# Two blocks of a transformer on one core: the second mixer's block attention reordered in pairs of units

## The reference, cut to what matters

```python
def second_block(x, ...):
    u = rms_norm(x, pre_mix_g[l]) @ w_in[l]
    u_conf, u_sc, u_att, u_lru = jnp.split(u, splits, axis=-1)
    y_a = conformer_conv_mixer(u_conf, ...)   # gated, 31-tap depthwise conv, group norm, silu
    y_b = short_conv_mixer(u_sc, ...)
    y_c = moba_attention(u_att)               # 4 heads of 64; softmax(q k - slope * distance) v
    y_d = rglru_mixer(u_lru, ...)             # conv, two gates, a linear recurrence, gelu
    y = jnp.concatenate([y_a, y_b, y_c, y_d], axis=-1) @ w_out[l]
    ...
```

## Time and profile before

| | us |
|---|---|
| median of 3 runs | 1278.79 (1278.21 to 1279.44) |
| the profiled execution | 1277.38 |
| its span, first to last instruction | 1275.6 |
| TensorE busy | 1267.5 |
| DVE busy | 741.4 |
| ACT busy | 569.3 |
| mean granted TensorE clock | 0.999 of full speed |

### The profile page before, as it was taken

The page is one execution under the profiler, slowest core; times in us unless marked ns, Lnnn a source line. Parts: engine busy times, 40 slices in busy tenths (PEclk is TensorE's granted clock), DMA queues, the critical chain, the costliest instruction groups (busy, mean ns, idle before and its releaser), DMA issues.

```text
span 1275.6 us, 15978 instructions
## 1 busy us (share of the span) xinstructions
PE 1267.5 (99%) x6406; PEld 1066.0 (84%) x6406; DVE 741.4 (58%) x1091; ACT 569.3 (45%) x974; POOL 7.0 (1%) x8
## 2 busy tenths in 40 slices
PE   9999999999999999999999999999999999999998
PEld 9877888898888888888888898778888888888886
DVE  5888876675586555555533589777653333433333
ACT  5666643344445444444422364576343322322222
POOL 0000010000000000000000000000000000000000
PEclk9999999999999999999999999999999999999999
DMA  8445446122224333233532052123243332333311
GB/s 257 141 165 191 139 129 221 65 83 66 101 82 133 99 99 98 91 94 97 164 93 92 32 159 93 51 67 118 80 134 99 99 95 91 115 96 99 99 50 66
DMA packets 43521, 138.54 MB, mean 109 GB/s; under 512 B 4628, under 2 KB 10260, under 8 KB 43192
## 3 DMA queue, kind: packets, MB, share of 16 engines
q1 hardware_dynamic: 43016, 137.13, 33.4%
q10 hardware_dynamic: 432, 0.39, 0.1%
HBM read 131.74 MB, written 5.77 MB: 108 GB/s over the span
## 4 chain that ended last, share of the span: by engine, by line
PE 88%; DMA 1%; DVE 0%; ACT 0%; issue 0%; DVEq 0%
PE bank L1295 15%; PE bank L1297 15%; PE bank L1296 15%; PE bank L1436 5%; PE bank L1437 5%; PE bank L1440 5%; PE bank L1438 5%; PE bank L1441 5%; PE bank L1439 5%; PE bank L1515 1%; PE bank L1579 1%; PE bank L1417 1%; PE bank L1416 1%; PE bank L1415 1%; PE bank L1565 1%; PE bank L1638 0%
## 5 line engine op out<-in xcount | busy, mean ns | idle before, releaser
L1295 PE MATMUL bank<-xh,whi 128*128 128x512 f32 (+1 forms) x1136 | 413.8, 364 | 0.0
L1296 PE MATMUL bank<-xl,whi 128*128 128x512 f32 (+1 forms) x1136 | 409.9, 361 | 0.0
L1297 PE MATMUL bank<-xh,wlo 128*128 128x512 f32 (+1 forms) x1136 | 409.8, 361 | 0.0
L2163 DVE TENSOR_TENSOR wlo<-stage,whi 128x1024 fp32r<-128x1024 f32 (+1 forms) x222 | 267.4, 1210 | 228.7 <-ACT whi L1698 228.5
L1698 ACT CAST whi<-stage 128x1024 fp32r<-128x1024 f32 (+1 forms) x222 | 228.5, 1036 | 199.4 <-PE bank L1441 157.2
L1295 PEld LDWEIGHTS bank<-xh,whi 128*128 128x128 f32 x1136 | 214.4, 189 | 36.9 <-issue 4.8
L1297 PEld LDWEIGHTS bank<-xh,wlo 128*128 128x128 f32 x1136 | 214.4, 189 | 32.6
L1296 PEld LDWEIGHTS bank<-xl,whi 128*128 128x128 f32 x1136 | 214.5, 189 | 32.1 <-issue 0.2
L1436 PE MATMUL bank<-whi,xh 128*128 128x512 f32 x281 | 110.3, 393 | 0.1
L1437 PE MATMUL bank<-whi,xh 128*128 128x512 f32 x281 | 109.4, 389 | 0.0
L1438 PE MATMUL bank<-wlo,xh 128*128 128x512 f32 x281 | 109.4, 389 | 0.0
(11 more groups left out here) (339 smaller groups left out, 1404.1 us busy)
## 6 DMA issues: line engine op xcount, KB each, us to landing
stage<-in_W_m SPq DMA_DIRECT2D x64, 512.0 KB, 3.6
stage<-in_W_up SPq DMA_DIRECT2D x44, 512.0 KB, 3.6
stage<-in_W_down SPq DMA_DIRECT2D x22, 512.0 KB, 3.6
stage<-in_W_in_a SPq DMA_DIRECT2D x19, 512.0 KB, 3.9
stage<-in_W_out SPq DMA_DIRECT2D x16, 512.0 KB, 3.7
stage<-in_W_in_b SPq DMA_DIRECT2D x10, 512.0 KB, 3.6
stage<-in_W_kv_k SPq DMA_DIRECT2D x8, 512.0 KB, 3.5
stage<-in_W_kv_v SPq DMA_DIRECT2D x8, 512.0 KB, 3.7
```

The source lines that it names most:

```text
L1295: e.matmul(b[:, cols], hi[:, k, :], xh[:, k, cols], start=(k == 0), stop=False)
L1296: e.matmul(b[:, cols], hi[:, k, :], xl[:, k, cols], start=False, stop=False)
L1297: last = e.matmul(b[:, cols], lo[:, k, :], xh[:, k, cols], start=False, stop=(k == 7))
L2163: e.tensor_tensor(wlo[:, plan.place[i], c], stage[:, i % NSTAGE, c], whi[:, plan.place[i], c].bitcast(F32), ALU.subtract).then_inc(S["w_lo"])
```

## The change

The step `mb_score` is taken apart into its three engines: `mb_score` (TensorE's matmuls), `mb_logit` (DVE) and `mb_exp` (ACT), which can now stand at different places in the list. A new method `mb_scores(u)` puts the matmuls of units u and u + 1 side by side and then the logits of u; the second unit's logits, the Exps, norms and transposes follow in later slots, and the two products with v stand side by side again. The taps are spread anew (the same 60 in the same order), `lru_gates(1)` goes from slot 22 to 23, and `lru_gates(0)`, `lru_a`, `lru_b` and `cf_mean` keep their slots. Nothing of the arithmetic is changed.

By slot, with the place in the main stream after which it stands (f and b: front and back half of a projection; gates, lru_a, lru_b and the other non-attention steps are shown where they stand beside attention):

| slot | after | before | after the change |
|---|---|---|---|
| 6 | in2_v tile 0 | score 0 | scores 0, 1; logit 0 |
| 7 | tile 1 | | logit 1; exp 0 |
| 8 | tile 2 | norm 0; score 1 | norm 0; exp 1 |
| 9 | tile 3 | | turn 0; norm 1 |
| 10 | in2_d 0 f | turn 0; norm 1; score 2 | turn 1 |
| 11 | in2_d 0 b | | pv 0, 1; scores 2, 3; logit 2 |
| 12 | in2_d 1 f | norm 2; turn 1; pv 0; score 3 | logit 3; exp 2 |
| 13 | in2_d 1 b | | norm 2; exp 3 |
| 14 | in2_b 0 f | norm 3; turn 2; pv 1; score 4 | turn 2; norm 3 |
| 15 | in2_b 0 b | norm 4 | turn 3 |
| 16 | in2_b 1 f | turn 3; pv 2; score 5 | pv 2, 3; scores 4, 5; logit 4 |
| 17 | in2_b 1 b | pv 3; norm 5 | logit 5; exp 4 |
| 18 | in2_b 2 f | gates 0; turn 4; score 6 | norm 4; gates 0 |
| 19 | in2_b 2 b | | exp 5 |
| 20 | in2_b 3 f | norm 6; turn 5; pv 4; score 7 | turn 4; norm 5 |
| 21 | in2_b 3 b, lru_gelu | | turn 5 |
| 22 | in2_b 4 f | pv 5; norm 7; turn 6; gates 1 | pv 4, 5; scores 6, 7; logit 6 |
| 23 | in2_b 4 b, sc_c 0 | | logit 7; exp 6; gates 1 |
| 24 | in2_b 5 f | pv 6; turn 7; lru_a | norm 6; exp 7; lru_a |
| 25 | in2_b 5 b, sc_c 1 | cf_parts; lru_b | turn 6; norm 7; cf_parts; lru_b |
| 26 | in2_b 6 f | pv 7 | turn 7 |
| 27 | in2_b 6 b | cf_mean | pv 6, 7; cf_mean |

Before, "score" stands for matmuls, logits and Exps together. Splits stand between slots as before: 146 ahead of in2_b 0, 147 and 148 behind lru_in 0 and 1, 149, 150 and 151 ahead of in2_b 3, 4 and 5.

```diff
@@ -775,11 +775,13 @@
         for q in range(2):
             self.step("cf_scale", q)
 
-    def mb_score(self, u):
-        for e in range(2):
-            self.fill("mb_score", u, e)
-            self.out(("mb_score", u, e), "mb_logit", 2 * u + e + 1)
-        self.step("mb_score", u)
+    def mb_scores(self, u):
+        for v in (u, u + 1):
+            for e in range(2):
+                self.fill("mb_score", v, e)
+                self.out(("mb_score", v, e), "mb_logit", 2 * v + e + 1)
+            self.step("mb_score", v)
+        self.step("mb_logit", u)
 
     def mb_turn(self, u):
         n = sum(MOBA_BANKS[:u])
@@ -822,82 +824,89 @@
         tap(3)
         yield
 
-        self.mb_score(0)
+        self.mb_scores(0)
+        tap(1)
+        yield
+        self.step("mb_logit", 1)
+        self.step("mb_exp", 0)
         tap(2)
         yield
+        self.step("mb_norm", 0)
+        self.step("mb_exp", 1)
         tap(3)
         yield
-        self.step("mb_norm", 0)
-        self.mb_score(1)
-        tap(2)
-        yield
-        tap(3)
-        yield
-
         self.mb_turn(0)
         self.step("mb_norm", 1)
-        self.mb_score(2)
+        tap(3)
+        yield
+        self.mb_turn(1)
+        tap(3)
+        yield
+
+        self.mb_pv(0)
+        self.mb_pv(1)
+        self.mb_scores(2)
+        tap(1)
+        yield
+        self.step("mb_logit", 3)
+        self.step("mb_exp", 2)
+        tap(3)
+        yield
+        self.step("mb_norm", 2)
+        self.step("mb_exp", 3)
+        tap(3)
+        yield
+        self.mb_turn(2)
+        self.step("mb_norm", 3)
+        tap(3)
+        yield
+        self.mb_turn(3)
+        tap(3)
+        yield
+
+        self.mb_pv(2)
+        self.mb_pv(3)
+        self.mb_scores(4)
+        tap(1)
+        yield
+        self.step("mb_logit", 5)
+        self.step("mb_exp", 4)
         tap(2)
         yield
+
+        self.step("mb_norm", 4)
+        self.lru_gates(0)
         tap(3)
         yield
-        self.step("mb_norm", 2)
-        self.mb_turn(1)
-        self.mb_pv(0)
-        self.mb_score(3)
-        tap(2)
-        yield
-        tap(4)
-        yield
-
-        self.step("mb_norm", 3)
-        self.mb_turn(2)
-        self.mb_pv(1)
-        self.mb_score(4)
-        tap(2)
-        yield
-        self.step("mb_norm", 4)
+        self.step("mb_exp", 5)
+        tap(3)
+        yield
+        self.mb_turn(4)
+        self.step("mb_norm", 5)
+        tap(3)
+        yield
+        self.mb_turn(5)
+        tap(3)
+        yield
+
+        self.mb_pv(4)
+        self.mb_pv(5)
+        self.mb_scores(6)
         tap(1)
         yield
-        self.mb_turn(3)
-        self.mb_pv(2)
-        self.mb_score(5)
-        tap(2)
-        yield
-        self.mb_pv(3)
-        tap(1)
-        self.step("mb_norm", 5)
-        yield
-
-        self.lru_gates(0)
-        self.mb_turn(4)
-        self.mb_score(6)
-        tap(2)
-        yield
-        tap(3)
-        yield
-        self.step("mb_norm", 6)
-        self.mb_turn(5)
-        self.mb_pv(4)
-        self.mb_score(7)
-        tap(3)
-        yield
-        tap(3)
-        yield
-
-        self.mb_pv(5)
-        self.step("mb_norm", 7)
-        self.mb_turn(6)
+        self.step("mb_logit", 7)
+        self.step("mb_exp", 6)
         self.lru_gates(1)
         tap(3)
         yield
-        tap(4)
-        yield
-        self.mb_pv(6)
-        self.mb_turn(7)
+
+        self.step("mb_norm", 6)
+        self.step("mb_exp", 7)
         self.step("lru_a")
         tap(4)
         yield
+        self.mb_turn(6)
+        self.step("mb_norm", 7)
         tap(60)
         self.keep("cf")
         for q in range(2):
@@ -906,8 +915,10 @@
         self.step("lru_b")
         yield
 
+        self.mb_turn(7)
+        yield
+        self.mb_pv(6)
         self.mb_pv(7)
-        yield
         self.cf_mean()
         yield
         self.step("lru_scan")
@@ -2012,7 +2023,7 @@
                 for z in range(2):
                     e.copy(av[:, 2 * z:2 * z + 2, :], tiles(bank_of("in2_v", z)[:], 2)).then_inc(S["v2_out"])
 
-            def mb_score(u):
+            def mb_exp(u):
                 w = 128 * (units[u][1] + 1)
                 q.wait_ge(S["mb_m"], u + 1)
                 for z in range(2):
@@ -2137,7 +2148,7 @@
                         warm=warm, xq=xq, xa_k=xa_k, xa_v=xa_v, xa_exp=xa_exp, xa_turn=xa_turn, decay=decay,
                         xa_pv=xa_pv, up=up, rms_stats=rms_stats, rms_late=rms_late, ln_apply=ln_apply, last_norm=last_norm, cf_in=cf_in, cf_first=cf_first, cf_parts=cf_parts, cf_mean=cf_mean,
                         cf_var=cf_var, cf_exp=cf_exp, cf_gate=cf_gate, in2_a=in2_a, in2_v=in2_v,
-                        mb_score=mb_score, mb_norm=mb_norm, mb_turn=mb_turn, lru_in=lru_in, lru_gate=lru_gate,
+                        mb_exp=mb_exp, mb_norm=mb_norm, mb_turn=mb_turn, lru_in=lru_in, lru_gate=lru_gate,
                         lru_a=lru_a, lru_b=lru_b, lru_gelu=lru_gelu, sc_c=sc_c, sc_conv=sc_conv,
                         post_norm=post_norm, m1=m1, store=store)
             e.dma_start(XT[:, 0, X0[0]], d["xT"][0][:, X0[0]]).then_inc(S["ld_xf"], 16)
@@ -2585,7 +2596,7 @@
                 e.scalar_tensor_tensor(out=yT[:, c, :], in0=cq[c], scalar=1.0, in1=cy[c], op0=ALU.add, op1=ALU.mult
                                        ).then_inc(S["cf_y"])
 
-            def mb_score(u):
+            def mb_logit(u):
                 p, i = units[u]
                 w = 128 * (i + 1)
                 Lq = Lm[u % 3][:, :, 0:w]
@@ -2712,7 +2723,7 @@
                         xq=xq, xa_k=xa_k, xa_v=xa_v, xa_turn=xa_turn, xa_score=xa_score, xa_norm=xa_norm, decay=decay, xa_pv=xa_pv, up_setup=up_setup, up=up, eps=eps,
                         rms_apply=rms_apply, rms_late=rms_late, gain=gain, ln_sums=ln_sums, ln_apply=ln_apply,
                         last_norm=last_norm, cf_in=cf_in, cf_tap=cf_tap, cf_parts=cf_parts, cf_mean=cf_mean, cf_scale=cf_scale,
-                        cf_out=cf_out, mb_score=mb_score, mb_norm=mb_norm, mb_pv=mb_pv, lru_in=lru_in, lru_a=lru_a,
+                        cf_out=cf_out, mb_logit=mb_logit, mb_norm=mb_norm, mb_pv=mb_pv, lru_in=lru_in, lru_a=lru_a,
                         lru_b=lru_b, lru_scan=lru_scan, sc_x=sc_x, sc_conv=sc_conv, sc_b=sc_b, post_norm=post_norm,
                         m1=m1)
             for name, *a in plan.steps:
```

More of the change, by code:

```diff
@@ L859, in beside_mixer_two @@
         self.step("mb_norm", 4)
+        self.lru_gates(0)
[14 more added lines that the diff above has]
+        self.mb_scores(6)
         tap(1)
         yield
-        self.mb_turn(3)
-        self.mb_pv(2)
-        self.mb_score(5)
-        tap(2)
-        yield
-        self.mb_pv(3)
-        tap(1)
-        self.step("mb_norm", 5)
-        yield
-        self.lru_gates(0)
-        self.mb_turn(4)
-        self.mb_score(6)
-        tap(2)
-        yield
+        self.step("mb_logit", 7)
+        self.step("mb_exp", 6)
+        self.lru_gates(1)
         tap(3)
@@ L879, in beside_mixer_two @@
         self.step("mb_norm", 6)
-        self.mb_turn(5)
-        self.mb_pv(4)
-        self.mb_score(7)
-        tap(3)
-        yield
-        tap(3)
-        yield
-        self.mb_pv(5)
-        self.step("mb_norm", 7)
-        self.mb_turn(6)
-        self.lru_gates(1)
-        tap(3)
-        yield
-        tap(4)
-        yield
-        self.mb_pv(6)
-        self.mb_turn(7)
+        self.step("mb_exp", 7)
         self.step("lru_a")
```

## The result

The changed kernel takes 1282.8 us (median of 6 runs, 1281.6 to 1284.4) against 1278.3 for the kernel before (6 runs beside it): ratio 1.0038, 95% interval 1.0028 to 1.0048. It is slower by 4.5 us; 4.9 had been forecast. Its profiled execution took 1281.8, with a span of 1280.0 against 1275.6.

The account below looks back on a forecast made before the run. TensorE, busy 99% of the span, bounds the kernel: waits 1.4 + 0.3 + 2.6 + 1.6 = 5.9, less 1.0 of switching, gives +4.9 on 1277.4: 1282.3, or 1283.7 us on the runs' median scale; range 1280.5 to 1287.0.

Parts of the forecast that it names:

- The waits of turns 5, 6 and 7: Second mixer: TensorE's transposes of units 5, 6 and 7 wait 1.4, 0.3 and 2.6 us for ACT's mb_norm.
- turns 2, 3 and 4: Transposes on TensorE's way to turn 5, counted at 0.54, 0.32 and 0.97 us within its 28.6.
- pv 7: Unit 7's product with v: TensorE waits 1.6 us for ACT's copy of turn 7, behind cf_parts and lru_b.
- The clock: Rival: TensorE's granted clock falls during a wait, the longest counted being 2.6 us; chance under 2 in 100.
- The row from the span's end: Profile row cited against the clock rival: granted clock at 2.4 GHz through four microseconds without a matmul.
- The switching: TensorE in the second mixer: pairing saves entries, less three more returns to the main stream; net -1.0 us.
- Entries: Cost on TensorE of entering a kind of work, paid once per run: 0.21 us for scores, 0.15 for products with v.
- All pairs together: Entries saved on TensorE by four score pairs and four v pairs: 1.44 us.
- The three returns: Main stream broken in 15 slots instead of 12: three more returns at 0.15 us each, 0.45 at most.

Follow-up runs that it names:

- e2_tail: Changed kernel with the last pair's steps (Exp, norm, turns and products of units 6 and 7) put forward; 1277.6 us, ratio 0.9997 to the kernel before.
- e3_unit5: Changed kernel with mb_norm(5) one slot earlier (slot 19, behind the second tap); 1280.4 us, ratio 1.0024 to the kernel before.
- e4_both: Changed kernel with the edits of e2_tail and e3_unit5 together; 1276.3 us, ratio 0.9985 to the kernel before.
- e5_lru_a_behind: Changed kernel with lru_a put behind norm 7 in slot 25, nothing else moved; 1285.5 us, ratio 1.0055 to the kernel before.
- e1_busy_wait: Changed kernel with nine extra 512-column matmuls in front of the wait of turn 7; 1282.1 us, ratio 1.0036 to the kernel before.
- e7_gelu_behind: e4_both with lru_gelu put behind the copy of turn 5 on ACT; 1275.5 us, ratio 0.9975 to the kernel before.

## Why the prediction was right

The time lay 0.9 us under the forecast, for the reason forecast: transposes that come too soon behind their scores for queues that run in order. By its steps:

- *The waits of turns 5, 6 and 7*: 1.93, 0.34 and 2.42 us, forecast 1.4, 0.3 and 2.6. At turn 5 ACT's side came as counted, 30.0 us after the end of in2_d 1 (801.78 to 831.79); TensorE would have been there after 27.9 instead of 28.6, and 0.5 of these 0.7 are turns 2, 3 and 4, which had been counted too long (see the switching below). e2_tail, e3_unit5 and e4_both took the waits away one by one, and the time followed. That the chain starts at the end of in2_b 4 and runs through lru_a is shown by e3_unit5 (unmoved when TensorE came earlier) and e5_lru_a_behind.
- *pv 7*: forecast 1.6. The wait is real, 1.40 in e1_busy_wait and e3_unit5 and 4.06 in e5_lru_a_behind, but in the changed kernel's profiled execution the half projection took 1.6 us longer at 1.2 GHz and the wait was covered.
- *The clock*, put at under 2 in 100: this step failed. The row from the span's end, four microseconds without a matmul at the upper level, was no safe witness, and it stops just short: in the same trace the clock falls 0.3 us behind the row's end, with no matmul between (the rows stand in the last section). It did little harm to the sum here, by the luck of pv 7's shadow. The upper runs of the changed kernel (1284.2 and 1284.4, mean granted clock 0.996 and 0.997 against 0.998 in the others) fit executions in which it fell once more in the open, but neither is in a trace; behind turn 5 (e1_busy_wait) and in the first mixer (e4_both) are two places where it was seen to.
- *The switching*: forecast -1.0, the term that was mis-sized. From the first token tile to the end of cf_mean TensorE took 83.3 us before and 80.8 without waits (e7_gelu_behind, 772.59 to 853.44): -2.5. Entries were as read (pairs of scores 1.71 instead of 1.06 + 0.85; of products 1.68 instead of 1.03 + 0.80). All pairs together saved 1.42 us, 1.44 had been counted. What was missed is in rows that the prediction used: eight transposes take 0.97 us up to the next start, four 0.54, and both stand ahead of another kind of side work. Now that they stand alone they take 0.79 (786.49 to 787.28) and 0.35 (804.51 to 804.86) up to the next main matmul: 0.14 to 0.18 less for seven units, and 0.06 for unit 7, whose transposes stood ahead of a main matmul before too (846.42 to 846.62), 1.2 us in all. The three returns, counted at 0.45, cost 0.16: from the first score to the end of pv 7, all that is not attention took 60.14 us before and 60.30 in e7_gelu_behind. That makes the 2.5.

So waits and clock came to 6.7 us where 5.9 had been counted (each piece by its starts against the same piece of e7_gelu_behind: 2.1 for turn 5, 0.5, 2.5, and 1.6 at the low clock), and the saving to 2.5 where 1.0 had been: two errors of about a microsecond that partly cancel, to 4.2, against 4.4 between the two spans. That the sum came so close is luck in part. They are not wholly apart: what the shorter transposes save ahead of turn 5 is given back there, since ACT sets when that wait ends.

## What to carry to other kernels

When work is regrouped on a full engine, count for each producer's queue what now stands between the input and the value waited for, from an event at which both queues last met; one unrelated step of 3.5 us in ACT's queue made a wait of 2.4, as much as all the regrouping saved. Moving that step alone only moves the wait to the next value behind it; bring every link forward, and the regrouping keeps its gain. And price a change of kind of matmul on both of its edges, where a group begins and where it ends.

## What the runs showed of the hardware

The granted clock of TensorE fell from 2.4 to 1.2 GHz after standstills much shorter than the prediction had thought safe, and not each time: after 2.42 us in the changed kernel but not after 2.40 in e3_unit5; after 1.93 us in e1_busy_wait but not after the same wait in the changed kernel; after 2.31 us in the first mixer of e4_both; after 4.06 us in e5_lru_a_behind. In the changed kernel, e1_busy_wait and e4_both the whole standstill is still at the upper level, and the clock fell 0.4 to 0.5 us after the matmuls had begun again; in e5_lru_a_behind it fell 0.5 us before they did. At the spans' ends, where no matmul follows, it fell 4.3 us after the last one in the kernel before, just behind the earlier trace rows, and 2.2 us after it in e2_tail. The kernel before:

```profile
1274.00:1274.50 0.50, 0.00 (x0) 0.00 (x0) 0.00 (x0) 0.00 (x0) 0.00 (x0) 0.79 1.03 342
1274.50:1275.50 1.00, 0.00 (x0) 0.00 (x0) 0.00 (x0) 0.00 (x0) 0.00 (x0) 0.50 0.13 42
```

The loss did not follow the length of the wait. The clock stayed low for 3.4 us in the changed kernel and in e1_busy_wait, which cost 1.6 us each (a half projection in 4.52 instead of 2.92), and for 6.8 us in e4_both and e5_lru_a_behind, which cost 3.1 and 2.9. What decides whether it falls, between two waits of one length, stays open.
